# A hybrid encoder step: two feed-forward stages cut at a chunk around output projections, entries to stages two slabs earlier, loops of small matmuls reordered

## What is computed

```python
h = x + 0.5 * rms_norm(swiglu(rms_norm(x, g1), w_in1, w_out1), g2)      # F1; D_FF = 2816
z = rms_norm(h, g3) @ w_in                                              # IP; 5376 columns
q, k, v, z_rw, z_g = split(z)
o_att = diff_attention(q, k, v, ...)      # 4 heads, two softmax maps, chunk mask or cache
o_rw = rwkv7_branch(z_rw, state, shift)   # 8 heads of 64, state update token by token
merged = sigmoid(z_gA) * (o_att @ w_o_att) + sigmoid(z_gB) * (o_rw @ w_o_rwkv)
h = h + rms_norm(merged @ w_out, g4)                                    # OP
y = h + 0.5 * rms_norm(swiglu(rms_norm(h, g5), w_in2, w_out2), g6)      # F2
```

## Time and profile before

| | us |
|---|---|
| median of 3 runs | 3148.43 |
| the profiled execution | 3144.15 |
| its span, first to last instruction | 3142.2 |
| PE busy | 3017.4 (96%) |
| DVE busy | 1725.4 (55%) |
| ACT busy | 1275.9 (41%) |
| POOL busy | 572.7 (18%) |
| mean granted clock | 0.982 |

### The profile page before, as it was taken

The page is one execution under the profiler, slowest core; times in us unless marked ns, Lnnn a source line. Parts: engine busy times, 40 slices in busy tenths (PEclk is TensorE's granted clock), DMA queues, the critical chain, the costliest instruction groups (busy, mean ns, idle before and its releaser), DMA issues.

```text
span 3142.2 us, 58552 instructions
## 1 busy us (share of the span) xinstructions
PE 3017.4 (96%) x23816; PEld 2674.4 (85%) x23816; DVE 1725.4 (55%) x2957; ACT 1275.9 (41%) x2602; POOL 572.7 (18%) x814
## 2 busy tenths in 40 slices
PE   8999999999999999999888999999999999999997
PEld 8998999888777888888777788878787889999997
DVE  5446445545344546465576745566566674456444
ACT  4334334444324443343344434344344453344333
POOL 1001000005115134150412305040310210000000
PEclk9999999999989999999999999999999999999999
DMA  5445444567447566353554536442433674445443
GB/s 168 127 127 173 139 125 149 180 195 234 132 124 253 172 186 186 105 156 89 187 175 134 184 112 193 120 151 83 138 118 120 221 228 131 126 148 165 126 128 121
DMA packets 499308, 481.62 MB, mean 153 GB/s; under 512 B 28521, under 2 KB 401537, under 8 KB 499025
## 3 DMA queue, kind: packets, MB, share of 16 engines
q1 hardware_dynamic: 470784, 387.48, 40.2%
q0 software_dynamic: 28256, 90.39, 9.4%
HBM read 430.57 MB, written 48.18 MB: 152 GB/s over the span
## 4 chain that ended last, share of the span: by engine, by line
PE 86%; DVE 6%; POOL 2%; issue 2%; DMA 2%; ACT 2%; SPq 0%; ACTq 0%; POOLq 0%; DVEq 0%
PE ps L246 39%; PE ps L256 29%; PE ps L996 5%; PE ps L1753 1%; PE ps L1687 1%; PE ps L1769 1%; DVE wlo L210 1%; PE ps L988 1%; PE ps L1001 1%; PE ps L1698 1%; PE ps L268 1%; PE ps L1154 1%; DVE as L1942 1%; PE ps L1763 1%; ACT whi L202 1%
## 5 line engine op out<-in xcount | busy, mean ns | idle before, releaser
L210 DVE TENSOR_TENSOR wlo<-raw,whi 128x512 fp32r<-128x512 f32 x1140 | 816.5, 718 | 888.3 <-ACT whi L202 886.4
L202 ACT ACTIVATE whi<-raw 128x512 fp32r<-128x512 f32 x1140 | 714.6, 629 | 670.1 <-PE ps L246 371.2
L246 PE MATMUL ps<-xnhi,whi 128*128 128x384 f32 x2688 | 927.3, 345 | 7.4 <-DVE xnlo L524 6.7
L246 PE MATMUL ps<-xnhi,wlo 128*128 128x384 f32 x2688 | 904.2, 336 | 0.0
L246 PE MATMUL ps<-xnlo,whi 128*128 128x384 f32 x2688 | 903.6, 336 | 0.0
L246 PEld LDWEIGHTS ps<-xnhi,whi 128*128 128x128 f32 x2688 | 508.9, 189 | 30.4 <-issue 14.8
L246 PEld LDWEIGHTS ps<-xnlo,whi 128*128 128x128 f32 x2688 | 508.8, 189 | 2.8 <-issue 2.2
L246 PEld LDWEIGHTS ps<-xnhi,wlo 128*128 128x128 f32 x2688 | 508.0, 189 | 0.0
L256 PE MATMUL ps<-whi,hidhi 128*128 128x512 f32 x936 | 379.2, 405 | 10.3 <-DVE xnlo L524 4.4
L256 PE MATMUL ps<-whi,hidlo 128*128 128x512 f32 x936 | 366.9, 392 | 0.0
L256 PE MATMUL ps<-wlo,hidhi 128*128 128x512 f32 x936 | 366.7, 392 | 0.0
(11 more groups left out here) (312 smaller groups left out, 3347.1 us busy)
## 6 DMA issues: line engine op xcount, KB each, us to landing
raw<-in_ffn_w_in_dram SPq DMA_DIRECT2D x528, 256.0 KB, 2.9
raw<-in_ffn_w_out_dram SPq DMA_DIRECT2D x264, 256.0 KB, 2.8
raw<-in_w_in_dram SPq DMA_DIRECT2D x252, 256.0 KB, 3.0
xt<-h_scratch SPq DMA_DIRECT2D x36, 512.0 KB, 6.1
att<-in_cache_att_k_dram POOLq DMA_DIRECT2D x64, 256.0 KB, 4.6
att<-in_cache_att_v_dram POOLq DMA_DIRECT2D x64, 256.0 KB, 3.3
rw<-zr_scratch POOLq DMA_DIRECT2D x51, 256.0 KB, 6.4
raw<-in_w_out_dram SPq DMA_DIRECT2D x48, 256.0 KB, 3.2
```

Of the source, the lines that this page charges most:

```text
L202: act.activation(B["whi"][:, slot], B["raw"][:, slot], ACT.Copy).then_inc(E["whi"], 1)
L210: dve.tensor_tensor(B["wlo"][:, slot], B["raw"][:, slot], B["whi"][:, slot].bitcast(F32), ALU.subtract).then_inc(E["wlo"], 1)
L246: ins = pe.matmul(ps[:, bank, 0:BT], B["w" + wt][:, n % RING, i * P:(i + 1) * P], x(xt, i), start=first and i == 0 and (wt, xt) == passes[ ...
```

## The change

The stages become F1 0, F1 1, IP 0, IP 1, F1 2, OP 0, IP 2, F2 0 with chunks 0 and 1, OP 1, F2 0 with chunk 2, F2 1 with chunks 0 and 1, OP 2, F2 1 with chunk 2, F2 2. Each of the 14 stages enters its input anew, so the norm before F2 0 and F2 1 is made twice. The partial sum in yb is stored to a new DRAM scratch, part, behind the first of the two stages ("spill"), and loaded back in the second from 10 slabs into it on ("refill"); chunk 2 is then added to what was loaded. The number of slabs stays 1140. LAST_OF_X, the positions of the counters ycopy and yadd, and the source of a stage's residual are taken from tables by stage instead of by kind.

Entries begin EARLY = 2 slabs sooner at every boundary that does not follow an IP stage; the pre steps move with them. In timetable the limits of the side work follow from the new places of OP 1 and OP 2.

In rw_pe four loops are reordered, with the same products: y_inner does the first product of both s before the second; SS takes pairs of heads and does the two first products, then the two second; UT has the loop over sequences outside that over heads; NS does all four quarters of the array in turn, both values of s together, and waits once ahead of them.

The diff, cut to its core. What is left out repeats the same replacements in the other engines' lists: fi * FT + j becomes unit(k, j), the loops over CHUNKS become loops over PARTS[k], the conditions of enter change as shown, and the norm lists step over spill and refill.

```diff
--- before.py
+++ after.py
@@ -38,13 +38,21 @@
 PRE = {"F1": 0, "IP": 8, "F2": 16}
 
 CHUNKS = [(0, 8), (8, 7), (15, 7)]
-STAGES = [("F1", 0), ("F1", 1), ("IP", 0), ("IP", 1), ("F1", 2), ("OP", 0), ("IP", 2), ("F2", 0), ("OP", 1), ("OP", 2), ("F2", 1), ("F2", 2)]
+WHOLE = (0, 1, 2)
+ORDER = [("F1", 0, WHOLE), ("F1", 1, WHOLE), ("IP", 0, ()), ("IP", 1, ()), ("F1", 2, WHOLE), ("OP", 0, ()), ("IP", 2, ()),
+         ("F2", 0, (0, 1)), ("OP", 1, ()), ("F2", 0, (2,)), ("F2", 1, (0, 1)), ("OP", 2, ()), ("F2", 1, (2,)), ("F2", 2, WHOLE)]
+STAGES = [(kind, blk) for kind, blk, _ in ORDER]
+PARTS = [part for _, _, part in ORDER]
 TILE_OF = [8, 0, 1, 2, 3, 4, 5, 6, 7]
-NSLAB = {"F1": 4 * FT + 2 * FT, "F2": 4 * FT + 2 * FT, "IP": 48 + 4 + 32, "OP": 32}
-FIRST = [sum(NSLAB[s] for s, _ in STAGES[:k]) for k in range(len(STAGES) + 1)]
-LAST_OF_X = {"F1": 4 * FT + 2 * (FT - CHUNKS[-1][1]), "F2": 4 * FT + 2 * (FT - CHUNKS[-1][1]), "OP": 16}
+SLABS = [{"IP": 48 + 4 + 32, "OP": 32}.get(kind, sum(6 * CHUNKS[c][1] for c in part)) for kind, _, part in ORDER]
+FIRST = [sum(SLABS[:k]) for k in range(len(STAGES) + 1)]
+LAST_OF_X = [{"IP": None, "OP": 16}[kind] if not part else n - 2 * CHUNKS[part[-1]][1] for (kind, _, part), n in zip(ORDER, SLABS)]
+TILES_AT = [sum(CHUNKS[c][1] for part in PARTS[:k] for c in part) for k in range(len(STAGES))]
+COPIES_AT = [6 * sum(c == 0 for part in PARTS[:k] for c in part) for k in range(len(STAGES))]
+ADDS_AT = [6 * sum(c > 0 for part in PARTS[:k] for c in part) for k in range(len(STAGES))]
 RING = 5
 AHEAD = 3
+EARLY = 2
 ROPE_AT, FLIP_AT = (0, 1, 5), (3, 4, 7)
 XP = ["aq", "ak", "r", "l", "k", "v", "av"]
 IP_ORDER = [("g", u) for u in range(4)] + [("x", pi) for pi in range(6)] + [("g", u) for u in range(4, 16)] + [("x", 6)]
...
+
+def entry(k):
+    return KT + (EARLY if STAGES[k - 1][0] != "IP" else 0)
+
+
+def spilled(k):
+    return bool(PARTS[k]) and PARTS[k][-1] != WHOLE[-1]
+
+
+def refilled(k):
+    return bool(PARTS[k]) and PARTS[k][0] != 0
+
+
+def unit(k, j):
+    return TILES_AT[k] + j - CHUNKS[PARTS[k][0]][0]
+
+
+def added(k, ci):
+    return ADDS_AT[k] + 6 * [c for c in PARTS[k] if c].index(ci)
+
+
+def source_of(kind, blk):
+    made = {"IP": "F1", "F2": "OP"}[kind]
+    return max(k for k, stage in enumerate(STAGES) if stage == (made, blk))
 
 
...
-                        if ci == len(CHUNKS) - 1 and inside(k) and hf * fn + i >= 2 * fn - 8:
-                            enter(k + 1, hf * fn + i - 2 * fn + 8)
+                        if ci == PARTS[k][-1] and inside(k) and 0 <= hf * fn + i - 2 * fn + 8 + EARLY < KT:
+                            enter(k + 1, hf * fn + i - 2 * fn + 8 + EARLY)
                         if i == fn - 1:
                             for tl in range(NT):
...
-                        enter(k + 1, kk)
+                    if inside(k) and 0 <= hf * KT + kk - KT + EARLY < KT:
+                        enter(k + 1, hf * KT + kk - KT + EARLY)
                     if kk == KT - 1:
                         for tl in range(NT):
                             bk.give(names[tl], "y2copy", oi * 6 + hf * 3 + tl + 1)
...
-                            enter(k + 1, hf * fn + i - 2 * fn + 8)
+                        if ci == PARTS[k][-1] and inside(k) and 0 <= hf * fn + i - 2 * fn + 8 + EARLY < KT:
+                            enter(k + 1, hf * fn + i - 2 * fn + 8 + EARLY)
                         if ci > 0 and i == fn - 1:
                             dve.wait_ge(E["used"], n + 1)
                             for tl in range(NT):
-                                if ci == 1:
-                                    dve.wait_ge(E["ycopy"], fi * 6 + hf * 3 + tl + 1)
+                                if ci == 1 and PARTS[k][0] == 0:
+                                    dve.wait_ge(E["ycopy"], COPIES_AT[k] + hf * 3 + tl + 1)
+                                elif ci == PARTS[k][0]:
+                                    dve.wait_ge(E["part_in%d" % tl], 16 * sum(refilled(i) for i in range(k + 1)))
                                 else:
-                                    dve.wait_ge(E["yadd"], fi * 12 + hf * 3 + tl + 1)
+                                    dve.wait_ge(E["yadd"], added(k, ci) - 6 + hf * 3 + tl + 1)
                                 y = B["yb"][:, tl, hf * 512:(hf + 1) * 512]
...
@@ -715,7 +748,9 @@
     seq = [("pre", 0)]
     for k in range(len(STAGES)):
         if k and STAGES[k - 1][0] != "IP":
-            seq.append(("post", k - 1))
+            seq.append(("spill" if spilled(k - 1) else "post", k - 1))
+        if refilled(k):
+            seq.append(("refill", k))
...
+MOVE_STEPS, REFILL_AT = 3, 10
 
 
 def norm_sp(sp, B, E, t):
     posts = pres = 0
     for what, k in norm_sequence():
         kind, blk = STAGES[k]
+        if what == "spill":
+            for tl in range(NT):
+                if PARTS[k] == (0,):
+                    sp.wait_ge(E["ycopy"], COPIES_AT[k] + 3 + tl + 1)
+                else:
+                    sp.wait_ge(E["yadd"], added(k, PARTS[k][-1]) + 3 + tl + 1)
+                at = NT * blk + tl
+                sp.dma_start(t["part"][at * P:(at + 1) * P], B["yb"][:, tl]).then_inc(E["hst%d" % tl], 16)
+                yield
+            continue
+        if what == "refill":
+            upto = nth(k, ("IP",)) * len(XP) * NT
+            for slot in range(6):
+                sp.wait_ge(E["zst%d" % slot], 16 * z_stores(slot, upto))
+            sp.wait_ge(E["turned"], ropes(upto))
+            for tl in range(NT):
+                sp.wait_ge(E["hst%d" % tl], 16 * nth(k, ("F1", "F2", "OP")))
+                at = NT * blk + tl
+                sp.dma_start(B["yb"][:, tl], t["part"][at * P:(at + 1) * P]).then_inc(E["part_in%d" % tl], 16)
+                yield
+            continue
         if what == "pre":
             if posts:
                 sp.wait_ge(E["h_done"], 3 * posts)
...
@@ -1114,6 +1183,7 @@
             for h in range(8):
                 for s in TWO:
                     pe.matmul(ps[half(s), RB[1], hn(h)], slot(S_QM + 1)[half(s), hx(h)], slot(S_U)[half(s), hx(h)], start=True, stop=False)
+                for s in TWO:
                     ins = pe.matmul(ps[half(s), RB[1], hn(h)], slot(S_QM + 2)[half(s), hx(h)], slot(S_V)[half(s), hn(h)], start=False, stop=True)
             ins.then_inc(E["rw_mm"], 1)
 
@@ -1130,10 +1200,15 @@
                 yield "US"
                 pe.wait_ge(*done(E, "u", 2 * tile + s + 1))
                 pe.wait_ge(*done(E, "y1", 2 * tile + s + 1))
-                for h in range(8):
-                    out = ps[half(h % 2), RB[0], h // 2 * 64:h // 2 * 64 + 64]
-                    pe.matmul(out, slot(S_BT)[half(s), hn(h)], slot(S_U)[half(s), hx(h)], start=True, stop=False, tile_position=(64 * s, 64 * (h % 2)))
-                    ins = pe.matmul(out, slot(S_KT)[half(s), hn(h)], slot(S_V)[half(s), hn(h)], start=False, stop=True, tile_position=(64 * s, 64 * (h % 2)))
+                for c in range(4):
+                    for x in TWO:
+                        h = 2 * c + x
+                        pe.matmul(ps[half(x), RB[0], c * 64:c * 64 + 64], slot(S_BT)[half(s), hn(h)], slot(S_U)[half(s), hx(h)],
+                                  start=True, stop=False, tile_position=(64 * s, 64 * x))
+                    for x in TWO:
+                        h = 2 * c + x
+                        ins = pe.matmul(ps[half(x), RB[0], c * 64:c * 64 + 64], slot(S_KT)[half(s), hn(h)], slot(S_V)[half(s), hn(h)],
+                                        start=False, stop=True, tile_position=(64 * s, 64 * x))
                 ins.then_inc(E["rw_mm"], 1)
                 if s:
...
@@ -1148,8 +1223,8 @@
                 yield "ST"
             pe.wait_ge(*done(E, "stT", 4))
             for bank, src in ((RB[0], S_V1), (RB[1], S_RF)):
-                for h in range(8):
-                    for b in range(NB):
+                for b in range(NB):
+                    for h in range(8):
                         par, c0 = half(h % 2), h // 2 * P
                         ins = pe.matmul(ps[par, bank, c0 + b * NQ:c0 + (b + 1) * NQ], slot(S_ST[b // 2])[par, c0 + b % 2 * 64:c0 + b % 2 * 64 + 64],
...
@@ -1166,16 +1241,18 @@
             yield "YY"
             for q in range(4):
                 pe.wait_ge(*done(E, "bk", 2 * q + 2))
-                for s in TWO:
-                    if q or s:
-                        pe.wait_ge(*done(E, "y", p + 1))
-                    if q:
-                        pe.wait_ge(*done(E, "ns", 2 * q - 1 + s))
-                    for h in range(8):
-                        out = ps[half(h % 2), RB[s], h // 2 * 64:h // 2 * 64 + 64]
-                        pe.matmul(out, slot(S_BK[0])[half(s), hn(h)], slot(S_U)[half(s), hx(h)], start=True, stop=False, tile_position=(64 * s, 64 * (h % 2)))
-                        ins = pe.matmul(out, slot(S_BK[1])[half(s), hn(h)], slot(S_V)[half(s), hn(h)], start=False, stop=True, tile_position=(64 * s, 64 * (h % 2)))
-                    ins.then_inc(E["rw_mm"], 1)
```

(40 more changed lines are left out.)

63 lines of the change are left out of this document (31 added, 32 removed).

## The result

The change makes the kernel 0.5% faster: 3130.27 us, median of 7 runs, beside 3145.34 for the kernel before, measured with it. One of the seven took 5282.90 us at a granted clock of 0.747 and is left out of the ratio, which compares the fast ones. The ratio is 0.9948 with a 95% interval from 0.9933 to 0.9963, so the gain is 16 us (12 to 21), where 56 were forecast. The forecast of 3092 and its range from 3045 to 3125 missed the time.

The account below looks back on a forecast made before the run. TensorE, with side matmuls and waits on side work, was taken to bound the kernel. Loops -14, entries -4.5, stages +9.2, spread -59, restarts +4, neighbours +8 sum to -56.3: 3148.43 to 3092 us, range 3045 to 3125.

Parts of the forecast that it names:

- The loops: Reordered side matmuls on TensorE alternate array quarters: UT 9.6, NS 3, SS with y_inner 1; -14 us, bounds -3 and -16.
- The entries: Next stage entered two slabs earlier: end wait goes, middle wait stays, 1.5 us at each of three boundaries, -4.5.
- Two more stages: Splitting F2 0 and F2 1 adds two entries with transposes behind OP 1 and OP 2, +9.2 us; spill and refill 0.
- Rival (a): New moves on SP's queue come late and TensorE pays for late weight loads: 3172 us, chance 4%.
- The spread: Side steps spaced wider over slabs: TensorE waits shrink 47 us and half clock 12, together -59.
- restarts: 34 more slabs hold a side step with TensorE work, each restart of dense matmuls costing about 0.1 us: +4.
- new neighbours: Side steps fall beside other steps, OP 1 now among them: +8 us, bounds 0 and +30.
- the five named waits: TensorE waits: X to T 15, C1 to O 7, P4 to FA 5, L1753 behind L1838 4, VA1 to ST 3.4 to go.
- The 12.6 us for lines with one or two cases: Added estimate for TensorE waits on lines not shown, part of the 47 us of waits to go.
- the 12 us for the clock: Eight half-clock stretches of TensorE vanish with the waits ahead of them, 1.5 us each.
- Rival (b): Waits do not go but move to new neighbours; only loops and entries remain: -5, 3143 us, chance 8%.
- Rival (c): Turned loops do nothing, the rate being that of weight loads and not of quarters: 3106 us, chance 12%.

Follow-up runs that it names:

- the old and the new places: Full change with side steps at the slabs of the kernel before (old), 0.9971 of the kernel before; full change as it is (new), 0.9948.
- both kinds of neighbours out of the way: Full change, LD steps sooner and normalisations last in a slab: 0.9833 in new places (VectorE's first attention wait also later), 0.9935 in old, against the kernel before.
- The loads: Full change with attention's LD steps 1 to 3 slabs sooner: 0.9886 of the kernel before; in the old places, up to three slabs sooner: 0.996.
- the order beside the normalisations: Full change with normalisation steps after side steps inside a slab on ScalarE, VectorE and GpSimd: 0.9896 of the kernel before, 3111.05 us.

## Why the prediction was wrong, step by step

- **What bounds the kernel** holds: TensorE sets the end, and moved side steps show in its waits alone.
- **The loops** were forecast at -14 and measured 10.7, as one layer. UT is L1229 now:

```profile
L1229 PE MATMUL ps<-rw 64*64 64x16 f32 x256 | 11.5, 240 | 0.0
```

It gained 8.1 us, 1.5 under the 9.6 taken: the step lies partly at the lower clock (0.50 from 883.4 to 897.1), so it ended between the bounds of 8.3 and 16.6. Three of the four NS steps take 1.16, as worked out, also behind a wait; the fourth takes 1.99, at half clock. From start to next start the four take 5.2 us, where they took 9.2 before, one of them at half clock. The wait grew from 5.0 to 6.6 us, so of the 3 us some 2.4 are left. Three of the NS steps:

```profile
910.71 1.99 PE L1252 MATMUL ps<-rw 64*64 64x64 f32 x64 [2.79 <-DVE rw L1540]
...
916.50 1.16 PE L1252 MATMUL ps<-rw 64*64 64x64 f32 x64
...
925.08 1.16 PE L1252 MATMUL ps<-rw 64*64 64x64 f32 x64 [1.32 <-DVE rw L1540]
```

SS gained nothing. The 0.035 of the forecast is the whole step up to the next matmul, 1.12 us for 32, and has the start and the end of the step in it. Inside the step the kernel before already ran faster:

```profile
1122.46 0.29 PE L1136 MATMUL ps<-rw 64*64 64x64 f32 x4
...
1123.16 0.33 PE L1136 MATMUL ps<-rw 64*64 64x64 f32 x4
```

Between these two starts lie 24 instructions, 0.029 us each. In the turned loop 20 of them take 1180.02 - 1179.43 = 0.59 us, 0.0295 each. So the loops come to 8.1 + 2.4 = 10.5 us by the traces. The forecast set the old NS against the token products by two different measures, too: from start to next start they take 1.94 and 2.01 us for 64.

By the rule of the Trainium skill that was weighed (TensorE: Matmul & The Clock Gate, The mechanism), a weight load overlaps running matmuls only where the row group differs, and SS gains nothing. That came out. The old NS, which by that rule should be slower than the token products, isn't (1.94 against 2.01 us).

- **The entries** behaved as described. At F1 0 to F1 1 the middle wait is still there and the first matmul of F1 1 has none in front (1.33 before):

```profile
277.52 0.47 PE L289 MATMUL ps<-whi,hidhi 128*128 128x512 f32 x1 [1.42 <-DVE xnlo L556]
...
293.72 0.33 PE L279 MATMUL ps<-xnhi,whi 128*128 128x384 f32 x1
```

-4.5 was forecast, 3 measured, and the intervals hold both 4.5 and none.

- **Two more stages** were forecast at +9.2 and measured some 4 us (5 either way), with spill and refill, whose 12 DMAs land in 2.7 to 9.3 us. No wait of VectorE's L603 (the old L570) for a DMA of the partial sums shows. Rival (a), late moves on SP's queue, didn't occur.
- **The spread** is the step that failed. It was -59 (47 waits, 12 clock) with +4 for restarts and +8 for new neighbours, -47 in all; measured 7. By the traces of the old and the new places 21 of the missing 40 us lie in waits that moved (the other rows were to shrink by 12.6 - 8 = 4.6 us and grew by 16.8), 10 in the five named waits, 9 in the clock; the restarts have no measurement of their own. Within it:
  - The five named waits that should shrink had terms of 15, 7, 5, 4 and 3.4, 34 us, and fell by 24.3. With both kinds of neighbours out of the way they shrank by 9.7, 8.3, 4.3, 5.2 and 2.3 between the two places, 29.8 us (a row that is missing counted as 0). These sizes were right then, but for X to T.
  - The 12.6 us for lines with one or two cases, an estimate without rows, had nothing behind it: all rows but the named five went from 49.5 to 51.1 us even then. In these kernels the single waits didn't vanish with density; others took their place.
  - The +8 for new neighbours was too small: the other rows grew by 16.8 us net. By the edits it is more. The loads took 20 us and the order beside the normalisations 16, in the new places; in the old ones the two took 4 and 8. That is some 24 us more in the new places, near the +30 that stood as the bound. The positions of LD, P1 and C2 could have been worked out from the timetable, as the distances within each branch were; the forecast said that LD to S stays 2 slabs both times (over all 12 pairs it is 1 in nine and 2 in three before, 1 in six and 2 in six after), and didn't look at what stands ahead of LD on GpSimd's queue.
  - Of the 12 us for the clock, 113 us at half clock down to 94 is at most 10 us for the whole change, UT included; the spread's own part is some 3 (100 down to 94).
- **The rivals.** Rival (b), waits that move to new neighbours, had 8% and gave 3143; on the median of 3145.34 its gain of 5 is 3140. It named the mechanism, but was written as if every us of the waits that go came back elsewhere, and with +9.2 for the two added stages. The time fell between it and the forecast. A rival worked out pair by pair would have deserved most of the chance. Rival (c), turned loops that do nothing, fell: UT and NS gained 10.5 us.
- **The range** had an error of its own at the low end: loops -16 and neighbours 0 give 3092 - 2 - 8 = 3082, not 3065. The high end, which the time missed, follows.

## What to carry to other kernels

When a schedule of fixed steps is stretched, the gain from longer distances within a chain is worth only what the new neighbours on each in-order queue leave of it: list, for every queue, which steps stand ahead of a DMA issue or of a link that the bounding engine waits for, in the new places as in the old. Issue loads as soon as their buffer is free, not in the slab that the timetable's proportion gives, and let work with long slack (here the normalisations) stand last in its slab. Try both before moving large parts: here they were worth 36 us on top of a change that alone brought 16.

## What the runs showed of the hardware

VectorE's instructions on two large inputs took longer beside GpSimd's large ones. L954 took 1.27 to 1.29 us in all 9 cases without any GpSimd work beside it, and just as long in 15 more, beside GpSimd's 128x1 instructions or, once, 0.15 us of a larger one. In the three cases beside GpSimd's 128x256 and 128x512 instructions of L1580 to L1582 it took 1.74, 2.30 and 2.31. L959 took 1.21 to 1.23 and once, beside the same lines, 2.82; GpSimd's L1580 took at most 1.30 alone and up to 1.74 beside VectorE. The row of L959 above is that case. The Trainium skill (GPSIMD Engine Reference, Specifications) says that GpSimd shares its SBUF interfaces with VectorE, with contention where a VectorE instruction has two SBUF inputs; L954 and L959 have two, and the trace agrees, with the size of GpSimd's instruction as a condition that the sentence doesn't name. So a large step of one branch on GpSimd is a neighbour of VectorE's list too, which wasn't in the forecast; no run here separates what it costs.
